# Last two experts of a mixture: input products first, other order of loads, the last tile in four pieces

## The chip, the cores and the metric

One core of a Trainium2 chip runs the whole computation. The metric is the device time of one execution in microseconds (us), taken as the median of several.

## The reference

Two transformer blocks run one after the other on 256 tokens of width 1024. The first, of two layers with convolution, latent attention and dilated attention, and the attention part of the second are not touched by the change. What matters is the mixture of experts that closes the second block, all in float32:

```python
N_EXPERTS, TOP_K, D_FF, D_MODEL = 32, 4, 1024, 1024
logits = xt @ w_router + b_router          # 256 tokens
top_val, top_idx = lax.top_k(logits, TOP_K)
gates = softmax(top_val)
# for each expert e, on the rows of the tokens that chose it:
hcat = xb @ w_in[e] + b_in[e]              # w_in[e]: 1024 x 2048
x_glu = minimum(hcat[:, :D_FF], 7.0)
x_lin = clip(hcat[:, D_FF:], -7.0, 7.0)
act = x_glu * sigmoid(1.702 * x_glu) * (x_lin + 1)
y_e = act @ w_out[e] + b_out[e]            # w_out[e]: 1024 x 1024
# weighted by its gate, y_e is added to its tokens; then residual and final norm
```

## The kernel before

The kernel goes through all 32 experts in order, whoever chose them, 64 rows for each. (Experts with more rows than 64 get a leftover job behind the others; the loop for it runs `n_jobs` times.) The weights of an expert come from HBM as six tiles of 2 MB: four of the input matrix (j = 0 to 3), each 16 KB per partition, and two of the output matrix (j = 4 and 5). They go into the six slots of `ring` (`MRING` = 6), slot j for tile j. All loads are issued by SyncE (SP) in `block_sync`; `expert(e, m, tiles)` issues the named tiles of expert e. Ahead of each it waits until the slot's last reader is done: for j = 0, 1, 2 and 4 on `mused` (TensorE adds one to it behind each of the first three input tiles and behind the first half of the output product), for j = 3 on `lin_done`, for j = 5 on `eout_done`. SP is in order, so an open wait holds every later load back. A landing adds 16 to `mlanded[j]`.

One expert is apart: expert 16 (`PARKED`). Its four input tiles are loaded long before, at the start of the stage, into held places outside the ring: `park` (two tiles), `pieces` (four quarters of the third, each where there is room) and `last_held` (the fourth). Their seven transfers add to one semaphore, `parked`, and TensorE waits for its whole count. In the ring the input tiles of expert 17 take the turn of expert 16's: SP issues 17's tiles 0 to 3, then 16's tiles 4 and 5, then 17's 4 and 5, and goes on with expert 18.

TensorE works by pairs of experts (`two_experts(i)`; `PAIRS` = 16), in this order:
1. `expert_in` of the even one: product of its rows with the input tiles, tile by tile as they land, each tile 16 matrix instructions in the profile (L1070), with the bias between the second and third tile (L1090); the fourth tile finishes first the glu half, then the linear half.
2. `scatter` of the pair before (L1131, adds its results to the token sums in the four banks), `turn_act` (transpose of the activation, L1117), `turn_sel` (transpose of the selection, L1124).
3. `expert_out` of the even one (L1108), 32 instructions, half 0 from slot 4 and half 1 from slot 5.
4. `expert_in` of the odd one; `gather(0)` (rows of the next pair, L1053), `turn_act`, `gather(1)`, `expert_out` of the odd one.

Between `expert_in` and `turn_act` DVE and ScalarE form the activation (`activate`); DVE copies the output product from its bank `mixed` (`expert_rows`, L1694 and L1695), before which the bank can't be written again. Behind expert 31 come the last scatter, the residual, the final norm and the store of the result.

Of the kernel before, what the change touches and what calls it, by code (L numbers as in the profile page):

```python
# [24 lines left out]
P = 128  # L25
T = 256
TT = T // P
D = 1024
# [182 lines left out]

PARKED, NPARK = PAIRS, 2
# [33 lines left out]
def build(nc, c_in, xT, ctxT, consts, layer_params, block_params, w_in, w_uq, w_ukv, w_out_a, w_out_b, w_out_c,  # L246
          w_o, w_ada, w_qkv, w_o2, e_in, eb_in, e_out, eb_out, out, sizes=None, debug=None):
    PER = sizes or CHAINED
    with ExitStack() as ctx:
# [316 lines left out]
        parked = sem("parked")  # L566
        mused = sem("mused")
# [128 lines left out]
        def block_sync(sp):  # L696
# [84 lines left out]
            expert(PARKED + 1, PARKED, range(HELD))  # L781
            expert(PARKED, PARKED, range(HELD, MRING))
            expert(PARKED + 1, PARKED + 1, range(HELD, MRING))
            with sp.Fori(PARKED + 2, NEXP) as e:
                expert(e, e)
            sp.wait_ge(table_ready, 2)
# [30 lines left out]
        def block_tensor(pe):  # L817
# [241 lines left out]
            def expert_in(m, hh, biased, here=False, behind=False):  # L1059
# [17 lines left out]
                for j in range(3):  # L1077
                    if here and j < HELD:
                        pe.wait_ge(parked, 16 * (NPARK + 4 + 1))
                    else:  # L1080
                        pe.wait_ge(mlanded[j], m * 16 + (0 if behind and j < HELD else 16))
                    for r in range(2):
                        for which in range(2):
                            ins = product(j, r, which)
                    ins.then_inc(mused, 1)
                    if j == 1:
                        pe.wait_ge(onehot_ready, biased)
                        for which in range(2):
                            for blk in range(2):
                                pe.matmul(score[HALF * blk:HALF * blk + HALF, which * W:(which + 1) * W],  # L1090
                                          onehot[:, hh, 2 * which + blk, :], bin_fold, start=False, stop=False)
                if not here:
                    pe.wait_ge(mlanded[3], m * 16 + (0 if behind else 16))
# [5 lines left out]
            def expert_out(m, hh):  # L1099
# [3 lines left out]
                for half in range(2):  # L1103
                    pe.wait_ge(mlanded[4 + half], m * 16 + 16)
                    for a in range(4):
                        for side in range(2):
                            blk = side if hh == 0 else 1 - side
                            ins = pe.matmul(mixed[HALF * side:HALF * side + HALF, :],  # L1108
                                            actT[:, hh, a * P + HALF * half:a * P + HALF * half + HALF],
                                            ring[:, 4 + half, a * D + blk * W:a * D + (blk + 1) * W],  # L1110
                                            start=half == 0 and a == 0, stop=half == 1 and a == 3)
                    ins.then_inc((mused, eout_done)[half], 1)
# [36 lines left out]
            def two_experts(i, first=False, here=False, behind=False):  # L1149
# [15 lines left out]
                expert_in(i * 2 + 1, 1, i + 1, behind=here or behind)  # L1165
# [7 lines left out]

            pe.wait_ge(bpar_loaded, 16 * (3 + FOLD))
# [3 lines left out]
            two_experts(PARKED // 2, here=True)  # L1178
            pe.wait_ge(table_ready, 2)
            n_jobs = pe.value_load(jobi[0:1, MAXJOBS:MAXJOBS + 1], min_val=0, max_val=MAXJOBS)  # L1180
            with pe.Fori(PARKED // 2 + 1, PAIRS) as i:
                two_experts(i, behind=True)
# [4 lines left out]
            with pe.If(n_jobs > 0):  # L1187
                with pe.Fori(0, n_jobs) as i:
# [6 lines left out]
                    expert_in(i + NEXP, 0, i + PAIRS + 1, behind=True)  # L1195
                    turn_act(i + NEXP, 0)
                    expert_out(i + NEXP, 0)
# [181 lines left out]
        def block_vector(dve, link, steps, base):  # L1379
# [324 lines left out]

            dve.wait_ge(table_ready, 2)
# [3 lines left out]
            with dve.Fori(1, PAIRS) as i:  # L1709
# [4 lines left out]
                assert steps[0] == PER["pair"], steps[0]  # L1714
            mark2 = mark + PAIRS * PER["pair"] + 1
# [1004 lines left out]
```

## Time and profile before

| what | us |
|---|---|
| median of 3 runs | 1948.62 |
| lowest and highest | 1946.19 and 1951.9 |
| profiled execution, its own time | 1951.37 |
| its span (first to last instruction) | 1949.6 |
| TensorE matmul busy | 1858.5 (95%) |
| DVE busy | 754.1 (39%) |
| ScalarE busy | 587.0 (30%) |
| moved by DMA | 563.39 MB |

Times in the rows are us from the start of the span. PE is TensorE's matrix work, PEld its weight loads, SP the engine that issues the DMAs, and SPq rows are its DMA issues. A matmul in float32 is several instructions, whose pipelined times overlap, so a group's busy time is read from its start to the start of the next. PEclk is the clock that TensorE was granted, 1.00 for 2.4 GHz and 0.50 for 1.2 GHz; in a stretch it is the mean.

### The profile page before, as it was taken

The page shows a single profiled execution, that of the slowest core. Times are in us where ns is not written, and L with a number is a line of the kernel's source. Part 1 is how long each engine was busy: PE and PEld are TensorE (multiplying, and loading weights), DVE is VectorE, ACT ScalarE, POOL GpSimd, SP SyncE. Part 2 cuts the span into 40 slices and gives each one's busy share as a digit, 9 for nine tenths or more (in the row PEclk, how much of TensorE's full clock was granted, in tenths as well). Part 3 has the DMA queues.
Part 4 walks back from the last instruction along what each step waited for, and adds up shares of the span by engine and source line. Part 5 has one row for each costly group of instructions (what it writes and reads, how often), then busy time and mean ns, then how long its engine had stood idle before and what let it go on. Part 6 is the DMA issues. An engine that isn't in the chain of part 4 may idle for free.

```text
span 1949.6 us, 26931 instructions
## 1 busy us (share of the span) xinstructions
PE 1858.5 (95%) x10980; PEld 1192.2 (61%) x10980; DVE 754.1 (39%) x1365; ACT 587.0 (30%) x1054; POOL 533.1 (27%) x224
## 2 busy tenths in 40 slices
PE   7999999989999899999989999999999999999997
PEld 6778989977789789957574444434434443343343
DVE  4775563446864543675543212112112211111112
ACT  4545455445545454444431001101101110110111
POOL 5767656767666457301000000000000000000000
PEclk9999999999999999999989999999999999999999
DMA  8554423556553333632579999999999999999995
GB/s 309 195 193 165 161 92 126 194 173 214 192 198 132 129 130 131 226 130 87 216 310 393 426 429 429 428 429 429 428 429 389 429 428 428 429 428 428 429 428 221
DMA packets 111989, 563.39 MB, mean 289 GB/s; under 512 B 4864, under 2 KB 24448, under 8 KB 87200
## 3 DMA queue, kind: packets, MB, share of 16 engines
q1 hardware_dynamic: 111904, 562.17, 72.3%
q8 instruction: 63, 1.03, 0.2%
q14 instruction: 22, 0.18, 0.0%
HBM read 561.11 MB, written 1.05 MB: 288 GB/s over the span
## 4 chain that ended last, share of the span: by engine, by line
PE 63%; DMA 28%; DVE 6%; ACT 1%; issue 1%; SPq 0%; DVEq 0%; ACTq 0%
DMA ring<-in_e_in_dram 26%; PE bank L1908 15%; PE score L1070 12%; PE bank L1898 10%; PE mixed L1108 4%; PE bank L1875 4%; PE bank L858 2%; PE bank L868 2%; PE mixed L1992 1%; PE flip L1975 1%; DVE ring L2499 1%; DMA ring<-in_e_out_dram 1%; PE bank L899 1%; PE score L1090 1%; PE bank L1131 1%
## 5 line engine op out<-in xcount | busy, mean ns | idle before, releaser
L2286 POOL TENSOR_TENSOR w_lo<-ring,w_hi 128x1024 fp32r<-128x1024 f32 (+1 forms) x216 | 523.3, 2434 | 277.4 <-ACT w_hi L2185 276.7
L1070 PE MATMUL score<-ring,space 128*64 128x512 f32 x1984 | 444.7, 594 | 33.9 <-DMA ring<-in_e_in_dram 32.7
L1070 PEld LDWEIGHTS score<-ring,space 128*64 128x64 f32 x1984 | 139.8, 137 | 327.8 <-issue 248.6
L2185 ACT ACTIVATE w_hi<-ring 128x1024 fp32r<-128x1024 f32 (+1 forms) x216 | 226.3, 1049 | 227.7 <-PE bank L1908 120.2
L1908 PE MATMUL bank<-h_hi,w_hi 128*128 128x256 f32 x896 | 261.6, 292 | 0.0
L1908 PE MATMUL bank<-h_lo,w_hi 128*128 128x256 f32 x896 | 253.4, 283 | 0.0
L1908 PE MATMUL bank<-h_hi,w_lo 128*128 128x256 f32 x896 | 252.0, 281 | 0.0
L1347 ACT ACTIVATE space<-space 128x512 f32<-128x512 f32 x32 | 20.2, 632 | 691.1 <-DVE space L1681 691.1
L1108 PE MATMUL mixed<-ring,space 128*64 128x512 f32 x1024 | 227.0, 595 | 0.9 <-DMA ring<-in_e_out_dram 0.7
L1681 DVE TENSOR_SCALAR space<-score 128x512 f32<-128x512 f32 x32 | 22.2, 693 | 402.6 <-PE score L1070 402.6
L1908 PEld LDWEIGHTS bank<-h_hi,w_hi 128*128 128x128 f32 x896 | 169.9, 190 | 4.6 <-issue 4.4
L1908 PEld LDWEIGHTS bank<-h_hi,w_lo 128*128 128x128 f32 x896 | 170.6, 190 | 0.0
L1908 PEld LDWEIGHTS bank<-h_lo,w_hi 128*128 128x128 f32 x896 | 170.4, 190 | 0.1
L1108 PEld LDWEIGHTS mixed<-ring,space 128*64 128x64 f32 x1024 | 70.6, 137 | 133.9 <-issue 129.9
L1898 PE MATMUL bank<-w_hi,h_hi 128*128 128x512 f32 (+1 forms) x320 | 131.6, 411 | 8.8 <-DVE h_lo L2348 8.8
L1694 DVE COPY space<-mixed 64x512 f32<-64x512 f32 x32 | 21.9, 684 | 297.1 <-PE mixed L1108 297.1
L1898 PE MATMUL bank<-w_lo,h_hi 128*128 128x512 f32 (+1 forms) x320 | 125.7, 393 | 0.0
L1898 PE MATMUL bank<-w_hi,h_lo 128*128 128x512 f32 (+1 forms) x320 | 125.2, 391 | 0.0
L1898 PEld LDWEIGHTS bank<-w_hi,h_hi 128*128 128x128 f32 x320 | 61.0, 191 | 26.2 <-issue 12.7
L1898 PEld LDWEIGHTS bank<-w_hi,h_lo 128*128 128x128 f32 x320 | 61.1, 191 | 12.6
L1898 PEld LDWEIGHTS bank<-w_lo,h_hi 128*128 128x128 f32 x320 | 61.3, 192 | 11.3 <-issue 0.5
L1131 PE MATMUL bank<-space 128*128 128x256 f32 x256 | 62.0, 385 | 1.5 <-DVE space L1695 1.5
(367 smaller groups left out, 2378.3 us busy)
## 6 DMA issues: line engine op xcount, KB each, us to landing
ring<-in_e_in_dram SPq DMA_DIRECT2D x124, 2048.0 KB, 25.0
ring<-in_e_out_dram SPq DMA_DIRECT2D x64, 2048.0 KB, 22.0
ring<-in_w_in_dram SPq DMA_DIRECT2D x42, 2048.0 KB, 7.8
ring<-in_w_ada_dram SPq DMA_DIRECT2D x16, 1024.0 KB, 5.3
ring<-in_w_o_dram SPq DMA_DIRECT2D x6, 2048.0 KB, 8.8
ring<-in_w_qkv_dram SPq DMA_DIRECT2D x4, 2048.0 KB, 9.8
ring<-in_w_ada_dram SPq DMA_DIRECT2D x4, 2048.0 KB, 9.7
ring<-in_w_out_a_dram SPq DMA_DIRECT2D x2, 2048.0 KB, 8.6
```

The source lines that it names most:

```text
L858: ins = pe.matmul(b[:, 0:n], (h, hc)[s_][:, c, cols], w8[:, c, 0:n], start=c == 0, stop=c == DC - 1)
L868: ins = pe.matmul(b[:, :], x_[:, c, cols], w_[:, c, :], start=c == 0 and x_ is x_hi and w_ is w_h, stop=c == DC - 1 and x_ is x_lo)
L1070: ins = pe.matmul(score[HALF * blk:HALF * blk + HALF, which * W:(which + 1) * W], xs[:, 2 * j + r, HALF * hh:HALF * hh + HALF], wk[:, blk ...
L1108: ins = pe.matmul(mixed[HALF * side:HALF * side + HALF, :], actT[:, hh, a * P + HALF * half:a * P + HALF * half + HALF], ring[:, 4 + half, ...
L1131: ins = pe.matmul(bank[c // 2][:, (c % 2) * T:(c % 2 + 1) * T], ys[:, c // 4, (c % 4) * P:(c % 4 + 1) * P], spread[:, c // 4, :], start=False,
L1681: dve.tensor_scalar(glu, score[:, 0:W], GLU_LIMIT, None, ALU.min).then_inc(glu_free, 1)
L1694: dve.tensor_copy(ys[0:HALF, hh, :], mixed[0:HALF, :])
L1875: ins = pe.matmul(b[:, i * T:(i + 1) * T], w_[:, c, m], y_[br][:, c, :], start=c == 0 and i == 0 and y_ is y_hi and w_ is hi, stop=c == 3 ...
L1898: ins = pe.matmul(b[:, 0:n], x_[:, c, t], w_[:, k % PARTS, i, 0:n], start=c == 0 and x_ is h_hi and w_ is w_hi, stop=c == DC - 1 and x_ is ...
L1908: ins = pe.matmul(b[:, half * T:(half + 1) * T], w_[:, k % PARTS, i, m:m + P], x_[:, c, :], start=c == 0 and half == 0 and x_ is h_hi and ...
L2185: act.activation(split_part(w_hi, k), raw_part(k), ACT.Copy).then_inc(hi_done, 1)
L2286: pool.tensor_tensor(split_part(w_lo, k), raw_part(k), split_part(w_hi, k), ALU.subtract).then_inc(lo_done, 1)
```

## The change

- **Order of loads at expert 16.** SP issues 17's tile 0, then 16's tiles 4 and 5, then 17's tiles 1 to 3, then 17's 4 and 5.
- **Loads of the last pair.** Expert 30's input tiles go to the ring as before. Then expert 31's four input tiles go to the held places that expert 16 has left (seven transfers, one semaphore `last_parked`), then expert 30's outputs into slots 4 and 5, then expert 31's outputs into slots 0 and 1 (`LAST_OUT`), freed by expert 30's input product; the last of them in four pieces of 0.5 MB with a semaphore each.
- **TensorE in the last pair** (`last_two`): expert 30's input product, scatter and transposes, expert 31's input product, first gather, expert 30's output product, transpose of 31's activation, second gather, expert 31's output product, whose second half waits piece by piece. Expert 31's input product begins with a wait for all of `last_parked`.
- **DVE in the last pair**: both activations, then the copies of both output products.
- Counts of `mlanded` in the leftover loop are adapted, since expert 31 doesn't use them.

```diff
--- before.py
+++ after.py
@@ constants, semaphores
+LAST, LAST_OUT = NEXP - 1, (0, 1)
+        last_parked = sem("last_parked")
+        last_piece = [sem(f"last_piece{i}") for i in range(5)]
...
@@ -778,11 +781,29 @@
             park_tile(1)
             with sp.Fori(1, PARKED) as e:
                 expert(e, e)
-            expert(PARKED + 1, PARKED, range(HELD))
+            expert(PARKED + 1, PARKED, range(1))
             expert(PARKED, PARKED, range(HELD, MRING))
+            expert(PARKED + 1, PARKED, range(1, HELD))
             expert(PARKED + 1, PARKED + 1, range(HELD, MRING))
-            with sp.Fori(PARKED + 2, NEXP) as e:
+            with sp.Fori(PARKED + 2, LAST - 1) as e:
                 expert(e, e)
+            expert(LAST - 1, LAST - 1, range(4))
+            sp.wait_ge(lin_done, PARKED + 1)
+            final = e_in[LAST].rearrange("(p j r) n -> p j (r n)", p=P, j=4)
+            for j in range(NPARK):
+                sp.dma_start(park[:, j, :], final[:, j, :]).then_inc(last_parked, 16)
+            for k in range(4):
+                sp.dma_start(pieces[k], final[:, NPARK, k * D:(k + 1) * D]).then_inc(last_parked, 16)
+            sp.dma_start(last_held, final[:, HELD - 1, :]).then_inc(last_parked, 16)
+            expert(LAST - 1, LAST - 1, range(4, MRING))
+            final = e_out[LAST].rearrange("(b p a) n -> p b (a n)", p=P, b=2)
+            sp.wait_ge(mused, LAST * 4 + 1)
+            sp.dma_start(ring[:, LAST_OUT[0], :], final[:, 0, :]).then_inc(last_piece[4], 16)
+            sp.wait_ge(mused, LAST * 4 + 2)
+            for a in range(4):
+                sp.dma_start(ring[:, LAST_OUT[1], a * D:(a + 1) * D], final[:, 1, a * D:(a + 1) * D]
+                             ).then_inc(last_piece[a], 16)
+            sp.wait_ge(eout_done, NEXP)
             sp.wait_ge(table_ready, 2)
             n_jobs = sp.value_load(jobi[0:1, MAXJOBS:MAXJOBS + 1], min_val=0, max_val=MAXJOBS)
             with sp.If(n_jobs > 0):
@@ -1056,7 +1077,7 @@
 
             glu_bank, lin_bank = score[:, 0:W], score[:, W:2 * W]
 
-            def expert_in(m, hh, biased, here=False, behind=False):
+            def expert_in(m, hh, biased, here=None, behind=0):
 
 
                 def product(j, r, which):
@@ -1076,9 +1097,9 @@
                 pe.wait_ge(lin_free, m + 1)
                 for j in range(3):
                     if here and j < HELD:
-                        pe.wait_ge(parked, 16 * (NPARK + 4 + 1))
+                        pe.wait_ge(here, 16 * (NPARK + 4 + 1))
                     else:
-                        pe.wait_ge(mlanded[j], m * 16 + (0 if behind and j < HELD else 16))
+                        pe.wait_ge(mlanded[j], (m - behind) * 16 + 16)
                     for r in range(2):
                         for which in range(2):
                             ins = product(j, r, which)
@@ -1090,24 +1111,29 @@
                                 pe.matmul(score[HALF * blk:HALF * blk + HALF, which * W:(which + 1) * W],
                                           onehot[:, hh, 2 * which + blk, :], bin_fold, start=False, stop=False)
                 if not here:
-                    pe.wait_ge(mlanded[3], m * 16 + (0 if behind else 16))
+                    pe.wait_ge(mlanded[3], (m - behind) * 16 + 16)
                 for which in range(2):
                     for r in range(2):
                         ins = product(3, r, which)
                     ins.then_inc((glu_done, lin_done)[which], 1)
 
-            def expert_out(m, hh):
+            def expert_out(m, hh, at=(4, 5), behind=0):
 
                 pe.wait_ge(act_in, m + 2)
                 pe.wait_ge(eout_free, m + 1)
                 for half in range(2):
-                    pe.wait_ge(mlanded[4 + half], m * 16 + 16)
+                    if at != LAST_OUT:
+                        pe.wait_ge(mlanded[4 + half], (m - behind) * 16 + 16)
+                    elif half == 0:
+                        pe.wait_ge(last_piece[4], 16)
                     for a in range(4):
+                        if at == LAST_OUT and half == 1:
+                            pe.wait_ge(last_piece[a], 16)
                         for side in range(2):
                             blk = side if hh == 0 else 1 - side
                             ins = pe.matmul(mixed[HALF * side:HALF * side + HALF, :],
                                             actT[:, hh, a * P + HALF * half:a * P + HALF * half + HALF],
-                                            ring[:, 4 + half, a * D + blk * W:a * D + (blk + 1) * W],
+                                            ring[:, at[half], a * D + blk * W:a * D + (blk + 1) * W],
                                             start=half == 0 and a == 0, stop=half == 1 and a == 3)
                     ins.then_inc((mused, eout_done)[half], 1)
 
@@ -1146,7 +1172,7 @@
                 ins = pe.matmul(mixed[0:NEXP, t * P:(t + 1) * P], gate[:, t, :], ident, start=True, stop=True)
             ins.then_inc(mixed_done, 1)
 
-            def two_experts(i, first=False, here=False, behind=False):
+            def two_experts(i, first=False, here=None, behind=0):
                 pe.wait_ge(rows_in, i * 2 + 2)
                 pe.wait_ge(act_in, i * 2 + 1)
                 expert_in(i * 2, 0, i + 1, here, behind)
@@ -1162,7 +1188,7 @@
                 turn_sel(i + 1)
                 expert_out(i * 2, 0)
 
-                expert_in(i * 2 + 1, 1, i + 1, behind=here or behind)
+                expert_in(i * 2 + 1, 1, i + 1, behind=1 if here else behind)
                 pe.wait_ge(spread_in, i + 2)
                 pe.wait_ge(sel_ready, i + 2)
                 gather(0, flip)
@@ -1171,15 +1197,38 @@
                 gather(1, lin_bank)
                 expert_out(i * 2 + 1, 1)
 
+            def last_two():
+                i = PAIRS - 1
+                pe.wait_ge(rows_in, i * 2 + 2)
+                pe.wait_ge(act_in, i * 2 + 1)
+                expert_in(LAST - 1, 0, i + 1, behind=1)
+                pe.wait_ge(spread_in, i + 1)
+                pe.wait_ge(eout_free, LAST)
+                scatter(range(0, 6))
+                turn_act(LAST - 1, 0)
+                scatter(range(6, DC))
+                turn_sel(i + 1)
+                pe.wait_ge(act_in, LAST + 1)
+                expert_in(LAST, 1, i + 1, here=last_parked)
+                pe.wait_ge(spread_in, i + 2)
+                pe.wait_ge(sel_ready, i + 2)
+                gather(0, flip)
+                expert_out(LAST - 1, 0)
+                turn_act(LAST, 1)
+                pe.wait_ge(lin_free, LAST + 2)
+                gather(1, lin_bank)
+                expert_out(LAST, 1, LAST_OUT)
+
             pe.wait_ge(bpar_loaded, 16 * (3 + FOLD))
             two_experts(0, first=True)
             with pe.Fori(1, PARKED // 2) as i:
                 two_experts(i)
-            two_experts(PARKED // 2, here=True)
+            two_experts(PARKED // 2, here=parked)
             pe.wait_ge(table_ready, 2)
             n_jobs = pe.value_load(jobi[0:1, MAXJOBS:MAXJOBS + 1], min_val=0, max_val=MAXJOBS)
-            with pe.Fori(PARKED // 2 + 1, PAIRS) as i:
-                two_experts(i, behind=True)
+            with pe.Fori(PARKED // 2 + 1, PAIRS - 1) as i:
+                two_experts(i, behind=1)
+            last_two()
 
             pe.wait_ge(eout_free, NEXP + 1)
             for i in range(DC // 2):
@@ -1192,9 +1241,9 @@
                     gather(1, lin_bank)
                     pe.wait_ge(rows_in, i * 2 + 2 * PAIRS + 4)
                     turn_sel(i + PAIRS + 1)
-                    expert_in(i + NEXP, 0, i + PAIRS + 1, behind=True)
+                    expert_in(i + NEXP, 0, i + PAIRS + 1, behind=2)
                     turn_act(i + NEXP, 0)
-                    expert_out(i + NEXP, 0)
+                    expert_out(i + NEXP, 0, behind=1)
                     pe.wait_ge(spread_in, i + PAIRS + 2)
                     pe.wait_ge(eout_free, i + NEXP + 2)
                     scatter(range(DC)).then_inc(scattered, 1)
@@ -1702,16 +1751,29 @@
                 activate(i * 2 + 1, 1)
                 expert_rows(i * 2 + 1, 1)
 
+            def last_two():
+                activate(LAST - 1, 0)
+                select(0, LAST + 1)
+                select(1, LAST + 2).then_inc(sel_ready, 1)
+                activate(LAST, 1)
+                expert_rows(LAST - 1, 0)
+                expert_rows(LAST, 1)
+
             dve.wait_ge(table_ready, 2)
             n_jobs = dve.value_load(jobi[0:1, MAXJOBS:MAXJOBS + 1], min_val=0, max_val=MAXJOBS)
             mark = steps[0]
             two_experts(0)
-            with dve.Fori(1, PAIRS) as i:
+            with dve.Fori(1, PAIRS - 1) as i:
                 base[0] = i * PER["pair"] + mark
                 steps[0] = 0
                 masks_of(i)
                 two_experts(i)
                 assert steps[0] == PER["pair"], steps[0]
+            base[0] = (PAIRS - 1) * PER["pair"] + mark
+            steps[0] = 0
+            masks_of(PAIRS - 1)
+            last_two()
+            assert steps[0] == PER["pair"], steps[0]
             mark2 = mark + PAIRS * PER["pair"] + 1
             with dve.If(n_jobs > 0):
```

## Rows read from the trace of the kernel before

**Rows 1.** The page: its first line, and GB/s in 40 slices of the span
```profile
span 1949.6 us, 26931 instructions
...
GB/s 309 195 193 165 161 92 126 194 173 214 192 198 132 129 130 131 226 130 87 216 310 393 426 429 429 428 429 429 428 429 389 429 428 428 429 428 428 429 428 221
```

**Rows 2.** Chain of waits, experts 30 and 31: start us, us, what
```profile
1861.32 25.42 DMA ring<-in_e_in_dram
...
1890.67 25.45 DMA ring<-in_e_in_dram
...
1916.16 3.68 PE score L1070 x16
...
1922.03 0.75 PE score L1117 x4
1922.78 1.79 PE score L1053 x16
1924.56 7.04 PE mixed L1108 x32
...
1933.08 3.72 PE bank L1131 x16
```

**Rows 3.** Transfers into the ring issued 1901 to 1904: the last output tile
```profile
L727 SPq DMA_DIRECT2D ring<-in_e_out_dram x1: 333/333/333, 1902.3 to 1902.3; - x1
...
DMA to landing us min/median/max: 23.6/23.6/23.6
```

**Rows 4.** Instructions in order of time, TensorE, expert 30 (start, us, what, idle)
```profile
1894.40 0.60 PE L1124 MATMUL flip<-cst,space 128*128 128x128 f32 x4
1894.93 7.09 PE L1108 MATMUL mixed<-ring,space 128*64 128x512 f32 x32
```

**Rows 5.** Instructions in order of time, TensorE, expert 16 from held places
```profile
1475.92 7.04 PE L1070 MATMUL score<-parked_tiles,space 128*64 128x512 f32 x32
...
1491.47 2.86 PE L1131 MATMUL bank<-space 128*128 128x256 f32 x12
...
1496.03 3.65 PE L1108 MATMUL mixed<-ring,space 128*64 128x512 f32 x16
1500.37 3.65 PE L1108 MATMUL mixed<-ring,space 128*64 128x512 f32 x16 [0.68 <-DMA ring<-in_e_out_dram]
```

**Rows 6.** Chain of waits, expert 18: the transpose with its input long ready
```profile
1549.48 0.47 PE score L1117 x4
```

**Rows 7.** Instructions in order of time, TensorE, behind an idle in layer one
```profile
416.58 0.69 PE L1898 MATMUL bank<-w_hi,h_hi 128*128 128x416 f32 x1 [4.93 <-DVE h_lo L2348]
```

**Rows 8.** Stretches: length, PE, PEld, DVE, ACT, POOL busy, PEclk, DMA share, GB/s
```profile
412.00:416.00 4.00, 0.00 (x0) 0.00 (x0) 3.96 (x6) 1.27 (x3) 1.94 (x1) 0.74 0.94 318
416.00:418.00 2.00, 1.42 (x4) 1.40 (x5) 2.00 (x3) 1.80 (x3) 1.43 (x1) 0.50 0.12 43
...
420.00:422.00 2.00, 1.53 (x7) 1.07 (x6) 2.00 (x3) 0.00 (x0) 0.76 (x1) 0.81 0.00 0
...
1008.00:1012.00 4.00, 2.36 (x11) 2.21 (x10) 1.56 (x11) 3.98 (x6) 0.00 (x0) 0.50 1.08 459
1012.00:1018.00 6.00, 4.90 (x23) 4.93 (x24) 3.37 (x16) 1.90 (x6) 0.00 (x0) 0.50 0.42 178
```

**Rows 9.** Issues of DMAs by SP around expert 16 (first start, us, what, count)
```profile
1450.08 14.68 SPq L727 DMA_DIRECT2D ring<-in_e_in_dram  x4
1472.76 31.69 SPq L727 DMA_DIRECT2D ring<-in_e_out_dram  x4
...
1499.79 0.33 SPq L727 DMA_DIRECT2D ring<-in_e_out_dram  x1
```

**Rows 10.** Stretches behind expert 16, the same columns as in rows 8
```profile
1497.00:1500.00 3.00, 2.69 (x14) 0.66 (x10) 0.00 (x0) 0.00 (x0) 0.00 (x0) 1.00 0.28 120
1500.00:1503.00 3.00, 2.63 (x13) 0.92 (x15) 0.00 (x0) 0.00 (x0) 0.00 (x0) 1.00 0.75 197
...
1506.00:1509.00 3.00, 3.00 (x16) 1.01 (x14) 0.00 (x0) 0.00 (x0) 0.00 (x0) 1.00 1.05 344
```

## Prediction

> **What bounds the kernel now.** I read the page first, then the chain of waits at the end of the run, then the instructions in order of time around expert 31 and around expert 16, then the clock and DMA share by stretches. The page shows 428 or 429 GB/s in nearly every slice of the second half, with one lower slice (389) [rows 1]. The chain explains it: every expert's fourth input tile is asked for when the slot is free and lands 25.4 us later, again and again, until expert 31's lands at 1890.67 + 25.45 = 1916.12 [rows 2]. Between expert 30's (1886.74) and expert 31's are 29.38 us for six tiles of 2 MB, 4.90 us each. So up to 1916 the transfers bound the time. After that TensorE does: one quarter product (3.68), the activation on DVE, the transpose (0.75), the second gather (1.79), the output product (7.04, to 1931.60), two copies on DVE, and the scatter from 1933.08 [rows 2]. The tail behind the output product is the same in both kernels. Expert 31's last output tile lands at 1902.3 + 23.6 = 1925.9 [rows 3], before its half of the product begins at about 1928. It isn't what ends last.
>
> **The load order of the last pair.** After the change SP asks for expert 30's four input tiles, expert 31's four (into the held places), 30's two outputs, then 31's two. The held places wait for nothing late (expert 16 has left them), so all are asked for right behind 30's fourth tile, at 1861.3, and no byte is added. The queue is full and stays full. Hence 31's inputs land one by one behind 1886.74 and the last of them at 1886.74 + 4 x 4.90 = 1906.3, 30's outputs at 1911.2 and 1916.1, 31's at 1921.0 and 1925.9 in four pieces.
>
> **What TensorE makes of it.** Today its work is spread: expert 30's output product (1894.93 to 1901.8) fills the wait for 31's inputs, and these are multiplied tile by tile as they land [rows 4]. After the change that output product stands behind all of 31's input product, and the input product begins with one wait for the whole count of the seven transfers. So TensorE has nothing from about 1895.0, where the selection's transpose ends [rows 4], to 1906.36, and then everything in one piece:
> - the whole input product, with its bias: expert 16's runs from held places with no wait, 1475.92 to 1491.47 [rows 5], so 15.55, to 1921.91;
> - first gather 1.79 [rows 2], to 1923.70; output product of 30, 7.04, to 1930.74;
> - transpose of 31's activation 0.47 where the activation was long ready, as it is here [rows 6], to 1931.21;
> - second gather 1.79, to 1933.00; output product of 31, 7.04, to 1940.04.
>
> Today this point is 1931.60, so **+8.4 us**. The transfers are all in at 1925.9; splitting the last tile in four buys nothing, since its product starts some ten microseconds later. On DVE, 30's copies from the output bank now stand behind 31's activation. They end 1.5 us behind the output product (1931.60 to 1933.08) [rows 2], at 1932.2, hidden by the second gather with 0.8 to spare; without that cover the excess would be added.
>
> **The clock.** The hole of 11.4 us is new: today TensorE starts its next product 0.5 us after the transpose [rows 4]. The nearest row: after TensorE's idle 4.93 us before 416.58 [rows 7] the granted clock was 0.74 in the stretch of the idle, 0.50 at the restart and 0.81 in 420 to 422 [rows 8]. A mean of 0.81 is 0.76 us at half clock, so the low level (1.2 GHz) lasted about 4.2 us into the new work, and half of it is lost: **+2.1 us**. Bounds: nothing, if the clock stayed; and 3.6, from the longest low stretch, 1008 to 1018, where 7.26 us of busy time ran at 0.50 [rows 8]. A gain is excluded, as idling can't lift the clock above 1.00. I take 2.1, since a complete idle is most like the first.
>
> The Trainium skill (TensorE: Matmul & The Clock Gate, Part 1: The HAM clock gate) says that half rate is the default state which sustained activity releases, and that idling brings it back. That speaks against this change; without such a fall the sum would be 2.1 lower, and the rows above agree with the rule.
>
> **The order at expert 16.** Today 17's four inputs are asked for from 1450.08 on, then 16's outputs from 1472.76 on [rows 9]. The second of these ends up late: 16's output product waits 0.68 us for it at 1500.37 [rows 5]. Then the queue runs dry, because 17's outputs need the slots that 16's output product frees (first issue 1499.79) [rows 9]: 120, 197 and 344 GB/s against 428 in three stretches of 3 us [rows 10]. That is (308 + 231 + 84) x 3 / 428 = 4.4 us of transfers lost. After the change 16's outputs stand behind only one tile of 17. They can't be asked for before 1472.76 (that is what frees the slot), when the queue is nearly empty (17's first tile, asked for at 1450.08, lands after some 25.4 us as others do [rows 2], at about 1475.5), so they land near 1481 and 1487, well ahead of 1496.03, and the 0.68 goes. The three other tiles of 17 then follow to about 1501 to 1503, before they are used. But the dry queue stays: TensorE is busy without a break from 1475.92 to 1499.7 on the parked expert, and only then frees the slot. So **-0.7 us**, passed on by a queue that is full from there on. Bounds: 0, if the two microseconds lost at 1473 come back as a later refill, and -4.4 if the whole hole closed; the release by TensorE puts it near the first.
>
> **Everything else.** The changed count in the leftover loop changes no work. Unrolling a pair adds instructions to fetch; expert 16's pair is written out too and starts without a gap at 1475.92 [rows 5], and at expert 30 the hole behind it would hide one. The seven issues and the five late ones on SP lie in a queue some 25 us ahead of the data, and what stands behind them on SP is only the store of the result.
>
> **Sum.** +8.4 + 2.1 - 0.7 = +9.8. On the profiled span 1949.6 gives 1959.4; that execution's own time was 1951.37, 1.8 above its span and 2.8 above the median of the three runs, 1948.62. I forecast from the median: 1958.4.
>
> **Rivals.**
> - *The clock doesn't fall* (or little): +8.4 - 0.7, 1956.3. Against it are the low stretches [rows 8]; for it, only that the fall is never at the same place of an idle. Chance 0.12.
> - *The hole at expert 16 closes*: 4.4 instead of 0.7, +6.1, 1954.7; together with a steady clock +4.0, 1952.6. It needs 17's outputs asked for before 1497, which TensorE's unbroken work speaks against. Chance 0.10.
> - *The end follows the transfers (faster)*: the last piece at 1925.9 and a quarter of half a product behind it (0.9) would end the output product at 1926.8, 4.8 sooner, with the 0.7 1943.1. This takes TensorE's work behind the inputs, 33.7 us, to begin by 1893.1; the change isn't slower only if all of 31's inputs are there before about 1898.7 (1906.4 less 8.4 - 0.7). They would have to overtake some two tiles of 4.90 us each in a full queue, or the wait to be for single tiles, which the code doesn't have. Chance 0.07.
> - *The change doesn't do what it says*: the inputs go late or SP is held up by so many open transfers, so that TensorE waits past 1906 by a tile, +14.7, 1963.3. At expert 16's side nothing of that size is seen. Chance 0.05.
>
> **How the numbers follow.** The forecast has 0.66. Range: 1952.5 (hole closed and clock steady) to 1962.5 (clock at its bound 3.6 and no gain at expert 16 give 1960.6, and the runs shown differ by some 2 to 3 us from their median); outside remain the faster rival and most of the last, about 0.12, and a little noise. About 0.3% (5.8 us) is what a measurement of this kernel tells from no change. Slower by more: forecast, first rival, half of the second, the last, less some noise: 0.84. Within: 0.09. Faster: 0.07.
>
> **What would show it.** In the profile after: one idle of TensorE of about 11 us before the last input product, put down to a transfer into a held place, at about 1905.6 in the new time; a granted clock of 0.5 just behind it; from there to the last output product no wait at all; the last out tile landed about 14 us before that product ends. At expert 16: no wait before 16's second output half, but still a dip to 120 to 200 GB/s near 1500. I'm wrong if the last input product starts before 1898.7, if the queue is full through 1500, or if an end of the last output product falls with the last piece.

## The result, and the profile after

| | before | changed |
|---|---|---|
| median, 6 runs each (us) | 1948.67 | 1960.18 |
| lowest and highest | 1945.87 and 1951.9 | 1956.79 and 1963.04 |
| span of the profiled execution | 1949.6 | 1959.9 |

The changed kernel is slower: the ratio is 1.0056, with a 95% interval of 1.0044 to 1.0067, which is 8.6 to 13.1 us. The forecast was 1958.4, or +9.8.

The page of the changed kernel, its first line and the lines of clock and transfers in 40 slices. They answer to [rows 1]: the second half is as full as before, and the last slices differ.

```profile
span 1959.9 us, 26867 instructions
...
PEclk9999999999999999999989999999999999999989
...
GB/s 308 194 193 176 147 111 120 205 179 193 201 172 170 89 130 172 222 91 86 274 282 416 428 429 428 428 428 428 428 428 393 428 429 428 428 429 428 428 426 124
```

TensorE's instructions in order of time in the last pair of the changed kernel (start, duration, what, and in brackets the idle before it and who ended it). They answer to [rows 2] and [rows 4].

```profile
1885.22 3.65 PE L1091 MATMUL score<-ring,space 128*64 128x512 f32 x16 [1.05 <-DMA ring<-in_e_in_dram]
...
1892.84 0.60 PE L1150 MATMUL flip<-cst,space 128*128 128x128 f32 x4
1905.12 9.94 PE L1091 MATMUL score<-parked_tiles,space 128*64 128x512 f32 x32 [11.69 <-DMA last_held<-in_e_in_dram]
...
1923.58 2.05 PE L1074 MATMUL flip<-space 128*128 128x128 f32 x16
1925.56 7.09 PE L1134 MATMUL mixed<-ring,space 128*64 128x512 f32 x32
1932.58 0.76 PE L1143 MATMUL score<-cst,space 128*128 128x128 f32 x4
1933.17 1.95 PE L1074 MATMUL score<-space 128*128 128x128 f32 x16
1935.05 7.09 PE L1134 MATMUL mixed<-ring,space 128*64 128x512 f32 x32
1943.64 3.72 PE L1157 MATMUL bank<-space 128*128 128x256 f32 x16 [1.50 <-DVE space L1744]
```

The reader is to see one idle of 11.69 us, ended by the transfer of the fourth held tile, and behind it no gap at all until the copies on DVE. From 1905.12 to about 1942.1 TensorE does both output products and a whole input product in a row. The input product, 1905.12 to 1923.58, takes 18.46 us, where the same instructions took 15.55 for expert 16 [rows 5].

Stretches of the changed kernel (length, busy time of PE, PEld, DVE, ACT, POOL, granted clock, DMA share, GB/s):

```profile
1896.00:1902.00 6.00, 0.00 (x0) 0.00 (x0) 0.00 (x0) 0.00 (x0) 0.00 (x0) 0.60 1.03 429
1902.00:1905.00 3.00, 0.00 (x0) 0.00 (x0) 0.00 (x0) 0.00 (x0) 0.00 (x0) 0.50 1.01 431
1905.00:1907.00 2.00, 1.88 (x6) 0.73 (x8) 0.00 (x0) 0.00 (x0) 0.00 (x0) 0.50 1.06 451
...
1909.00:1911.00 2.00, 2.00 (x6) 0.53 (x4) 0.00 (x0) 0.00 (x0) 0.00 (x0) 0.52 1.00 426
1911.00:1913.00 2.00, 2.00 (x12) 0.77 (x10) 0.00 (x0) 0.00 (x0) 0.00 (x0) 1.00 0.96 410
...
1920.00:1925.00 5.00, 5.00 (x30) 2.50 (x27) 1.98 (x3) 0.63 (x1) 0.00 (x0) 1.00 0.62 246
1925.00:1930.00 5.00, 5.00 (x28) 2.02 (x28) 0.69 (x1) 1.51 (x4) 0.00 (x0) 1.00 0.00 0
```

In the idle the granted clock fell to 0.50 (1.2 GHz) and stayed there for the first 5.8 us of the new work. Half of that is 2.9 us, just what the input product took too long. The transfers are over by 1925 (the last piece was asked for at 1895.2 and landed 29.6 us later), some 17 us before the last output product ends.

At expert 16 of the changed kernel, its output product in TensorE's instructions in order of time:

```profile
1495.63 7.09 PE L1134 MATMUL mixed<-ring,space 128*64 128x512 f32 x32
```

And its stretches there, with the same columns as above: the one in which 16's output tiles are asked for, and two that answer to [rows 10].

```profile
1472.00:1477.00 5.00, 5.00 (x26) 1.72 (x24) 1.25 (x2) 0.00 (x0) 0.00 (x0) 1.00 0.86 311
...
1497.00:1500.00 3.00, 3.00 (x18) 1.00 (x16) 0.00 (x0) 0.00 (x0) 0.00 (x0) 1.00 0.53 224
1500.00:1503.00 3.00, 3.00 (x18) 1.00 (x16) 0.24 (x1) 0.00 (x0) 0.00 (x0) 1.00 0.84 262
```

The output product runs in one piece, so the wait of [rows 5] has gone. The queue still runs thin: (204 + 166) x 3 / 428 = 2.6 us near 1500 and 117 x 5 / 428 = 1.4 us near 1475, together 4.0 where it was 4.4. Most of the hole was only split and moved.

### The profile page after: what moved, and what is told of

It reads as the page before. It is cut to its first block, busy times and chain, and to the rows that moved or that the text cites. A ratio compares the mean times of both kernels' runs of the same rounds, so it can differ in the third digit from the quotient of the medians.

```text
span 1959.9 us, 26867 instructions
## 1 busy us (share of the span) xinstructions
PE 1861.6 (95%) x10980; PEld 1194.9 (61%) x10980; DVE 753.4 (38%) x1365; ACT 586.3 (30%) x1054; POOL 533.7 (27%) x224
## 4 chain that ended last, share of the span: by engine, by line
PE 66%; DMA 25%; DVE 6%; ACT 1%; issue 1%; SPq 1%; DVEq 0%; ACTq 0%
DMA ring<-in_e_in_dram 22%; PE bank L1970 15%; PE score L1091 13%; PE bank L1960 10%; PE mixed L1134 5%; PE bank L1937 4%; PE bank L879 2%; PE bank L889 2%; DMA last_held<-in_e_in_dram 2%; PE mixed L2054 1%; PE bank L920 1%; DVE ring L2561 1%; PE flip L2037 1%; PE score L1111 1%; PE bank L1157 1%
## 5 line engine op out<-in xcount | busy, mean ns | idle before, releaser
L1091 PE MATMUL score<-ring,space 128*64 128x512 f32 x1920 | 430.0, 594 | 32.5 <-DMA ring<-in_e_in_dram 31.4
L1091 PEld LDWEIGHTS score<-ring,space 128*64 128x64 f32 x1920 | 135.6, 137 | 316.2 <-issue 242.1
```

The lines of the kernel that those rows point to most:

```text
L1091: ins = pe.matmul(score[HALF * blk:HALF * blk + HALF, which * W:(which + 1) * W], xs[:, 2 * j + r, HALF * hh:HALF * hh + HALF], wk[:, blk ...
```

## The experiments

Single executions of one kernel differ by more than most of the effects: those of the kernel before lay between 1945.3 and 1954.7, its medians at 1948.67, 1949.81 and 1948.61 in the three series of executions. The changed kernel was timed in the first series; the next four experiments with a ratio are from the second, those without gathers from the third, and each ratio is to the kernel before in its own series. Much of the scatter lies ahead of expert 15: its last quarter product starts anywhere from 1456.6 to 1463.3 in these profiles. So besides the times I read two distances from that start (1460.67 in the kernel before, 15.25 ahead of the first line of [rows 5]): to expert 29's last quarter product, which tells of expert 16, and to the last scatter, which tells of everything. The last column is their difference, from expert 29's last quarter product to the last scatter, which tells of the last pair alone.

| kernel | order at 16 | wait in 16's output product | to expert 29 | to last scatter | from 29 to it |
|---|---|---|---|---|---|
| before | old | 0.68 | 396.76 | 472.41 | 75.65 |
| before, second profile | old | 0.31 | 395.82 | 471.47 | 75.65 |
| last pair alone | old | 0.30 | 395.49 | 483.00 | 87.51 |
| new order at 16 alone | new | 0 | 395.80 | 471.48 | 75.68 |
| changed | new | 0 | 395.52 | 483.37 | 87.85 |
| changed, last tile whole | new | 0 | 395.58 | 483.34 | 87.76 |
| changed, filler | new | 0 | 395.39 | 480.58 | 85.19 |
| tile waits | new | 0 | 395.28 | 469.29 | 74.01 |
| tile waits, no gathers | new | 0 | 395.46 | 468.27 | 72.81 |
| the same, last tile whole | new | 0 | 395.46 | 469.55 | 74.09 |

Expert 29's last quarter product, first in the kernel before, then in the changed one:

```profile
1857.43 3.65 PE L1070 MATMUL score<-ring,space 128*64 128x512 f32 x16 [1.00 <-DMA ring<-in_e_in_dram]
```
```profile
1855.79 3.65 PE L1091 MATMUL score<-ring,space 128*64 128x512 f32 x16 [0.99 <-DMA ring<-in_e_in_dram]
```

The last column repeats well: 75.65, 75.65 and 75.68 in the three profiles whose last pair is the old one. In it the changed kernel loses 12.2 us.

**The new order at expert 16 alone**

```diff
-            expert(PARKED + 1, PARKED, range(HELD))
+            expert(PARKED + 1, PARKED, range(1))
             expert(PARKED, PARKED, range(HELD, MRING))
+            expert(PARKED + 1, PARKED, range(1, HELD))
```

> The kernel before with the new order of loads at expert 16 and nothing else. Read between the start of expert 15's last quarter product and that of expert 30's, which is 426.11 us in the kernel before and 424.95 in the changed one. My theory (the slot of expert 17's outputs is freed by TensorE's unbroken work on the parked expert, so only the wait for expert 16's second output tile goes): 424.9 to 425.5, time 0.7 to 1.2 lower than before, within what the runs tell from no change. Rival (the hole of the queue at expert 16 closes): 421.7, time 4.4 lower. Second rival (the 1.2 us in the changed kernel come from somewhere else): 426.1, no change.

Measured: ratio 0.9992 to before, interval 0.9983 to 1.0001 (a gain of 3.3 to a loss of 0.2 us). From expert 15 to expert 30 it has 1882.02 - 1456.84 = 425.18.

```profile
1456.84 3.65 PE L1071 MATMUL score<-ring,space 128*64 128x512 f32 x16 [0.99 <-DMA ring<-in_e_in_dram]
...
1492.20 7.09 PE L1109 MATMUL mixed<-ring,space 128*64 128x512 f32 x32
...
1882.02 3.65 PE L1071 MATMUL score<-ring,space 128*64 128x512 f32 x16 [0.98 <-DMA ring<-in_e_in_dram]
...
1928.32 3.72 PE L1132 MATMUL bank<-space 128*128 128x256 f32 x16 [1.50 <-DVE space L1696]
```

The first rival falls: the hole would have had to bring 421.7. Whether my theory holds, or the second rival (no gain here at all), depends on the next two.

**The last pair alone, old order at expert 16** (the diff above the other way round, in the changed kernel)

> The changed kernel with the loads at expert 16 in the order of before. My theory (the whole loss lies in the last pair, 37.0 us from expert 31's input product to the end of its output product after the hole): 426.1 us between the last quarter products of experts 15 and 30, from the start of expert 31's input product to the end of its output product 37.0, and the time 11 to 13 above before, 1 more than the changed kernel. Rival (the new order at expert 16 costs something in the run that the chain does not show): less than 10 above before.

Measured: ratio 1.0072, interval 1.0051 to 1.0093, so about 14 us (10 to 18) above before. One of its six executions carries this: it took 1971.86 us at a mean granted clock of 0.937, the other five 1959.4 to 1964.1 at 0.987 to 0.989. The medians, 1960.97 and 1949.81, are 11.2 apart, within the 11 to 13 expected. TensorE's instructions in order of time:

```profile
1494.21 7.39 PE L1133 MATMUL mixed<-ring,space 128*64 128x512 f32 x32
...
1883.99 3.65 PE L1090 MATMUL score<-ring,space 128*64 128x512 f32 x16 [1.24 <-DMA ring<-in_e_in_dram]
...
1903.90 9.38 PE L1090 MATMUL score<-parked_tiles,space 128*64 128x512 f32 x32 [11.69 <-DMA last_held<-in_e_in_dram]
...
1921.80 2.05 PE L1073 MATMUL flip<-space 128*128 128x128 f32 x16
...
1941.85 3.72 PE L1156 MATMUL bank<-space 128*128 128x256 f32 x16 [1.50 <-DVE space L1743]
```

The whole loss is there without the new order (87.51 in the last column of the table, 87.85 in the changed kernel). From 1903.90 to the end of the output product (1.5 before the scatter, 1940.35) are 36.5 us, 0.5 under the 37.0 expected, because the input product took 17.90 and not 18.46: the clock came back sooner (mean 0.86 in the stretch 1908 to 1910, 1.00 from there on, so about 4.7 us of work at 0.50, where it was 5.8). But the stretch from expert 15 to 30 was 1883.99 - 1458.85 = 425.14, and not the 426.1 that I expected of the old order. The wait in 16's output product was 0.30 here (7.39 for the group that takes 7.09 without one). That miss is why the next run was made.

**The kernel before, a second profile**

> The kernel before, unchanged, for a second profile: how far two executions of the same kernel lie apart in the same stretch. Between the last quarter products of experts 15 and 29 the first profile of it has 396.76 us, the changed kernel 395.52, the new order at expert 16 alone 395.80, the last pair alone (old order) 395.49. If the new order really gives 0.7 to 1.2 us, this one has 396.2 or more; if the old order also gives 395.5, the gain at expert 16 is lost in the difference between executions.

Measured, in a single execution: 395.82 to expert 29. TensorE's instructions around it:

```profile
1457.13 3.65 PE L1070 MATMUL score<-ring,space 128*64 128x512 f32 x16 [0.99 <-DMA ring<-in_e_in_dram]
...
1492.49 7.40 PE L1108 MATMUL mixed<-ring,space 128*64 128x512 f32 x32
...
1852.95 3.65 PE L1070 MATMUL score<-ring,space 128*64 128x512 f32 x16 [1.00 <-DMA ring<-in_e_in_dram]
...
1928.60 3.72 PE L1131 MATMUL bank<-space 128*128 128x256 f32 x16 [1.50 <-DVE space L1695]
```

The same kernel differs by 0.94 from one profile to the next. Three profiles of the old order give 396.76, 395.82 and 395.49, seven of the new one 395.28 to 395.80, mean 395.50: half a microsecond less in the mean. The wait in 16's output product was 0.68, 0.31 and 0.30. (The 0.68 is the idle that the profile gives; by the length of the whole group, as the other two are read, it is 1500.37 + 3.65 - 1496.03 = 7.99 against 7.09, or 0.90.) So the first profile overstated the wait: the same kernel had a third of it in the next. That the wait goes with the new order is shown, by seven profiles that have none. That the time gains by it is not: this second profile of the old order and the one of the new order alone have the same distances to 0.02 us (395.82 and 471.47, 395.80 and 471.48), the third of the old order lies inside those of the new, and only the first profile stands out. The gain at expert 16 is between nothing and about a half, and this run's expectation (396.2 or more if it is really 0.7 to 1.2) failed. The second rival of the run with the new order alone, no gain, stays open.

**Filler in the hole**

```diff
+                for _ in range(12):
+                    pe.matmul(mixed[:, :], ones, bin_fold, start=True, stop=True)
                 pe.wait_ge(act_in, LAST + 1)
                 expert_in(LAST, 1, i + 1, here=last_parked)
```

> The changed kernel with 12 matrix products of constants into the free output bank ahead of expert 31's input product, about 10 us of work that ends before the inputs are there; their result is overwritten. My theory (the granted clock falls in the hole of 11.7 us, and that costs 2.9 us of the 18.5 that the input product took): the clock stays at 1.00, the input product takes 15.6 instead of 18.5, and the output product ends 2.9 earlier; the time is 2.9 below the changed kernel, 8.6 above before. Rival (the input product is slow because the transfers write while TensorE reads, or for its operands' places): 18.5 as before, the same time as the changed kernel. The clock alone must not give back more than 3.

Measured: ratio 1.0043 to before, interval 1.003 to 1.0057; median 1957.12, 7.3 above before in its series, where the changed kernel has 11.5. The two intervals overlap, so it is the distances that decide. TensorE's instructions in order of time:

```profile
1889.67 10.46 PE L1212 MATMUL mixed<-cst,ones 128*128 128x512 f32 x24
1901.52 7.09 PE L1091 MATMUL score<-parked_tiles,space 128*64 128x512 f32 x32 [1.39 <-DMA last_held<-in_e_in_dram]
...
1917.12 2.05 PE L1074 MATMUL flip<-space 128*128 128x128 f32 x16
...
1937.18 3.72 PE L1157 MATMUL bank<-space 128*128 128x256 f32 x16 [1.50 <-DVE space L1746]
```

A stretch at the start of the input product, with the columns of the stretches above; the granted clock is 1.00:

```profile
1902.00:1904.00 2.00, 2.00 (x12) 0.84 (x10) 0.00 (x0) 0.00 (x0) 0.00 (x0) 1.00 1.04 442
```

Ten microseconds of useless work bring the end nearer. The input product takes 15.60 us from the same places, beside the same transfers, so neither the operands' places nor the writing beside it made it slow; the clock did. The distance to the last scatter is 2.79 shorter. What remains over before, 480.58 less 471.94 (the mean of its two profiles) = 8.6 us, is the wait together with the order, less what differs at expert 16. In the last pair alone it is 85.19 - 75.65 = 9.5 us: the 8.4 of the forecast, 0.5 by which the work is longer than forecast, and 0.6 by which the input product starts later behind expert 29 (1901.52 - 1851.99 = 49.53, where the forecast has 1906.36 - 1857.43 = 48.93).

**A wait for each held tile**

```diff
-        last_parked = sem("last_parked")
+        held_in = [sem(f"held_in{i}") for i in range(HELD)]
...
+                    if here is held_in:
+                        pe.wait_ge(held_in[j], 64 if j == NPARK else 16)
-                    if here and j < HELD:
+                    elif here:
                         pe.wait_ge(here, 16 * (NPARK + 4 + 1))
...
+                if here is held_in:
+                    pe.wait_ge(held_in[HELD - 1], 16)
...
```

> The changed kernel, but each of expert 31's four held tiles has a semaphore of its own, and TensorE waits for one tile at a time, as it does in the ring; the order of loads and of products stays. My theory (the one wait for all seven transfers makes the hole, the hole lowers the clock, and both input and output products then stand in a row behind the last input): expert 31's input product starts at about 1893.4 on the changed kernel's scale and ends at 1909, no wait over 1.5 us, the granted clock stays 1.00, expert 30's output product waits for its second tile (about 1914.6) and ends at 1918.1, and expert 31's output product ends at 1927.4 instead of 1942.2, limited by TensorE and a few us behind the last piece. The time is 14.8 below the changed kernel and 3 to 4 below before: 1945. Rival (the order of the products is what costs, whatever the wait): less than 5 below the changed kernel, above before.

Measured: ratio 0.9985 to before, interval 0.9974 to 0.9995, so 1 to 5 us faster. The median, 1947.27, is 2.5 under before in its series, where 3 to 4 were expected. The changed kernel is 11.5 above before in its own, so the two are 14.0 apart, where 14.8 were expected. TensorE's instructions in order of time:

```profile
1894.21 0.60 PE L1154 MATMUL flip<-cst,space 128*128 128x128 f32 x4
1894.74 7.09 PE L1091 MATMUL score<-parked_tiles,space 128*64 128x512 f32 x32
...
1910.35 2.05 PE L1074 MATMUL flip<-space 128*128 128x128 f32 x16
1912.33 3.65 PE L1138 MATMUL mixed<-ring,space 128*64 128x512 f32 x16
1916.22 3.65 PE L1138 MATMUL mixed<-ring,space 128*64 128x512 f32 x16 [0.23 <-DMA ring<-in_e_out_dram]
...
1922.27 7.09 PE L1138 MATMUL mixed<-ring,space 128*64 128x512 f32 x32
1930.85 3.72 PE L1161 MATMUL bank<-space 128*128 128x256 f32 x16 [1.50 <-DVE space L1748]
```

This is the run that decides. Order of loads, order of products, pieces and places are those of the changed kernel; only the wait is split. The input product begins 0.53 us after the selection's transpose, with no idle, takes its 15.6 us at a granted clock of 1.00, and the last scatter stands 14.1 us nearer to expert 15 (469.29 against 483.37) than in the changed kernel, and 2 to 3 nearer than before. Of these, 1.6 are in the last pair (74.01 against 75.65); the rest is at expert 16 and between executions. The rival, that the order itself costs, falls: with waits by tile it gains. It is a version that beats both kernels, the kernel before by little.

**The last tile whole, in the changed kernel**

```diff
-            for a in range(4):
-                sp.dma_start(ring[:, LAST_OUT[1], a * D:(a + 1) * D], final[:, 1, a * D:(a + 1) * D]
-                             ).then_inc(last_piece[a], 16)
+            sp.dma_start(ring[:, LAST_OUT[1], :], final[:, 1, :]).then_inc(last_piece[0], 16)
...
-                        if at == LAST_OUT and half == 1:
-                            pe.wait_ge(last_piece[a], 16)
+                        if at == LAST_OUT and half == 1 and a == 0:
+                            pe.wait_ge(last_piece[0], 16)
```

> The changed kernel with expert 31's last output tile in one transfer of 2 MB instead of four pieces. My theory (the second half of expert 31's output product starts over ten us after the tile has landed): no wait of the output product for it, and the same 37.0 us from the start of expert 31's input product to the end of its output product. Rival (the pieces are what the end waits for): a wait of 1 to 4 us before the second half.

Measured, in a single execution: the distance to the last scatter is 483.34 against 483.37, and the output product is one group with no wait. The input product took 18.30. Splitting is worth nothing there, at most 0.1.

```profile
1937.23 7.09 PE L1132 MATMUL mixed<-ring,space 128*64 128x512 f32 x32
```

**Tile waits, and the last pair's gathers left out**

The gathers select rows for experts 32 and 33, which don't exist; leaving them out changes nothing of the result.

```diff
-                gather(0, flip)
+                pe.sem_inc(gathered_half, 1)
                 expert_out(LAST - 1, 0)
                 turn_act(LAST, 1)
                 pe.wait_ge(lin_free, LAST + 2)
-                gather(1, lin_bank)
+                pe.sem_inc(gathered_half, 1)
```

> The kernel with a wait for each held tile, and both gathers of the last pair left out: they select rows for experts 32 and 33, which there are not, and the leftover loop gathers for itself. Only their semaphore is raised. My theory (the end is now limited by turns: expert 30's second output tile lands at 1916.2 on the scale of the kernel with tile waits, its product ends at 1919.8, the copies of its bank on DVE at 1921.3, and the last piece lands at 1926.0): expert 30's output product gets no faster, expert 31's starts at 1921.3 instead of 1922.3 and ends at 1928.4 instead of 1929.3; the time is 1 below the kernel with tile waits, about 4 below before. Rival (TensorE's work alone is the bound, two gathers of 1.8 each): 3.6 below.

Measured: the last scatter 1.02 nearer than with tile waits (468.27 against 469.29; 1.20 in the last pair), as expected and not 3.6. The freed time turns into waits, which stand in brackets:

```profile
1913.00 3.65 PE L1138 MATMUL mixed<-ring,space 128*64 128x512 f32 x16 [0.98 <-DMA ring<-in_e_out_dram]
1917.80 3.65 PE L1138 MATMUL mixed<-ring,space 128*64 128x512 f32 x16 [1.14 <-DMA ring<-in_e_out_dram]
1921.39 0.75 PE L1147 MATMUL score<-cst,space 128*128 128x128 f32 x4
1923.00 7.09 PE L1138 MATMUL mixed<-ring,space 128*64 128x512 f32 x32 [0.87 <-DVE space L1748]
```

The time doesn't confirm the last microsecond: the ratio to before is 0.9992, interval 0.998 to 1.0004, which takes in both the kernel with tile waits and no change. That this version is the fastest is shown of its last pair, not of whole runs.

**The same, and the last tile whole**

> The same without the gathers, and with expert 31's last output tile in one transfer. My theory (the split pays where the last tile is what the output product waits for, and gives the part of the half product that can be done before the last piece): a wait of about 1.3 us before the second half, the output product ends 1.2 later than with the pieces. Rival (smaller transfers of 4 KB a partition cost what they save): the same time or less.

Measured: a wait of 0.91 before the second half and the last scatter 1.28 later than with the pieces (469.55 against 468.27); ratio 0.9999, interval 0.999 to 1.0009. Here, where the output product does wait for the last tile, the pieces pay.

```profile
1921.63 3.65 PE L1136 MATMUL mixed<-ring,space 128*64 128x512 f32 x16 [0.86 <-DVE space L1746]
1926.19 3.65 PE L1136 MATMUL mixed<-ring,space 128*64 128x512 f32 x16 [0.91 <-DMA ring<-in_e_out_dram]
```

## Why the prediction was right, step by step

- **The landings.** The last held tile was forecast at 1906.3 less 0.7 at expert 16, or 1905.6; it landed at 1904.99. That it looks early is luck of this profile, in which expert 15 came 0.4 sooner and the stretch to expert 29 was 1.2 shorter; behind expert 29's last quarter product it landed 49.20 later (from 1855.79), where the forecast has 48.91 (1906.34 less 1857.43), so 0.3 late. Why is open. The queue was full up to the last tile, as forecast.
- **The hole.** Forecast 11.4 us, measured 11.69 in the changed kernel and in the last pair alone, 11.70 with the last tile whole. That the one wait makes it is shown by the tile waits, where it is gone.
- **All work in a row.** From the start of the input product to the end of the last output product the sum had 33.68 us at full clock; with filler it was 1901.52 to 1935.68 (1.50 ahead of the scatter), or 34.2. The half microsecond is mostly in two small terms: 0.47 for the transpose was taken from a place where nothing stood before it in the way that an output product does here (0.69), and the first gather took 1.98 instead of 1.79.
- **The clock.** This is the term of the sum that was mis-sized, though within its bounds of 0 and 3.6: forecast 2.1, measured 2.91, 2.35 and 2.75 in three executions (18.46, 17.90 and 18.30 less 15.55). The row that I took it from had an idle of 4.93 us and 4.2 us of low clock behind it, here 5.8 us followed an idle of 11.7, and 4.7 and 5.5 us in the two other executions, behind the same idle. The Trainium skill (TensorE: Matmul & The Clock Gate, Part 1: The HAM clock gate) has idling bring back half rate and sustained activity end it; the run with filler, where the idle is filled and the clock stays at 1.00, agrees, at 2.8 us.
- **Expert 16.** Forecast -0.7; the runs show a gain between nothing and about a half. Two parts of the mechanism were right: the wait in 16's output product went, and the hole stayed, as TensorE's work on the parked expert holds the slots. The size came from one wait in one profile, in the next two profiles that wait was 0.3, and that its removal is passed on to the end isn't shown. The dip near 1500 was shallower than I said (224 and 262 GB/s, not 120 to 200), since part of it moved to 1475.
- **The pieces.** Forecast nothing, measured 0.03. The last one landed 17 us before the last output product ended; 14 was forecast, the rest is the longer work behind the hole and the earlier start of this profile's last experts.
- **The copies on DVE.** Forecast hidden by the second gather; the output product behind it starts without a wait at 1935.05. With the gathers gone it waits 0.87 for them: the cover was needed.
- **The sum.** +8.4 + 2.1 - 0.7 = +9.8 was forecast; the medians differ by 11.5. In the last pair alone the profiles differ by 87.85 - 75.65 = 12.2, and the terms with measured sizes give it: 8.4 + 0.5 (work) + 2.9 (clock) + 0.4 (the input product starts 49.33 behind expert 29's last quarter product and not 48.93) = 12.2. With the 0 to 0.5 at expert 16 that is 11.7 to 12.2. All four terms fell short on the same side, each by under 1 us: no error hid another.

Of the rivals, a steady clock, a closed hole, and an end that follows the transfers did not come about. The third was the nearest to something real: it named waits for single tiles as its condition, and with them the kernel is faster than before. The fourth, that SP is held up by so many open transfers, named something that did happen (the last section has it), but without the tile's delay that it foresaw: the landings were 0.3 us late, not 4.9.

## What to carry to other kernels

When transfers are consumed as they land, one count for a group of them moves all their work behind the last of them; ask of each such wait what would be left to do at that moment, and sum it. Loading inputs early pays only if the work on them can start early too. An idle hole costs twice, once in time and once in the clock of the work behind it, and splitting a transfer helps only where the reader is already waiting for it.

## What the runs showed of the hardware that was not expected

SP's issue of a transfer, 0.33 us as a rule, took over 4 us here when many were open. These are two of SP's issues in the changed kernel, in order of time (start, duration, what); the second is the last held tile, which landed 35.2 us later:

```profile
1865.51 4.24 SPq L796 DMA_DIRECT2D space<-in_e_in_dram  x1
1869.79 4.24 SPq L797 DMA_DIRECT2D last_held<-in_e_in_dram  x1
```

The first slow issue (3.65 us, at 1861.82 in the chain of waits) met some nine open transfers: expert 29's last tile, 30's four, two held tiles and two pieces, counted from landings 4.90 us apart. The issues of the output tiles, up to the last piece, came in turn behind it. It cost nothing here, because the data lay 25 us and more behind the issues. Had SP had anything urgent behind it, that would presumably have waited too; no run has such a transfer. Whether the limit is one of transfers or of their parts wasn't tried.

The other is small: pieces of 0.5 MB, 4 KB a partition, cost the queue next to nothing. In four pieces the last tile landed 5.0 to 5.1 us behind the tile before it (1896.6 + 29.45 against 1884.2 + 36.9 with tile waits, 1895.2 + 29.6 against 1882.8 + 36.9 in the changed kernel), in one transfer 4.9 (1888.6 + 37.6 against 1884.3 + 37.0 without gathers, last tile whole).
